# Half of the expert-row sum on TensorE, and expert 1's first weight chunks called in the routing stage

## The reference

```python
logits = (xt @ p['w_router'] + p['b_router']).astype(F32)
top_val, top_idx = lax.top_k(logits, TOP_K)                 # TOP_K = 4
gates = jax.nn.softmax(top_val, axis=-1)
...
def expert_block(args):
    e, x_b = args
    gu = x_b @ w_gu[e] + b_gu[e]
    gate = jnp.minimum(gu[..., ::2], SWIGLU_LIMIT)
    up = jnp.clip(gu[..., 1::2], -SWIGLU_LIMIT, SWIGLU_LIMIT)
    return ((up + 1.0) * (gate * jax.nn.sigmoid(SWIGLU_ALPHA * gate))) @ w_dn[e] + b_dn[e]
...
y = jnp.zeros((T + 1, D)).at[slot_tok].add(yb * slot_g[:, None])[:T]
```

## Time and profile before

| | us |
|---|---|
| median of 3 timed runs | 2890.73 |
| lowest, highest | 2877.65, 2892.95 |
| the profiled execution, its own time | 2882.36 |
| its span (first to last instruction) | 2880.6 |
| of it: expert turns, TensorE from 1167.3 to 2222.2 | 1054.8 |
| of it: the sum's stage, 2227.7 to 2280.3 | 52.5 |

### The profile page before, as it was taken

How to read it: one execution, slowest core, us unless ns; L and a number is a source line. 1 busy time by engine, 2 the same in 40 slices (tenths; PEclk the granted TensorE clock), 3 DMA queues, 4 the chain that set the end, 5 groups by cost and what they waited for, 6 DMA issues and landing times. The chain is left out here.

```text
span 2880.6 us, 62057 instructions
## 1 busy us (share of the span) xinstructions
PE 2493.6 (87%) x23388; PEld 1218.8 (42%) x23388; DVE 1253.4 (44%) x2324; ACT 694.8 (24%) x1558; POOL 453.0 (16%) x384
## 2 busy tenths in 40 slices
PE   5888888856889996799999998999898699789998
PEld 3456565645564443233333332333233254455444
DVE  2263747463257426344444444544454512643012
ACT  3133333343061013111111111121111411354000
POOL 0031213130070000211111111111110101154000
PEclk8998989878899997899999999999999699989999
DMA  6000000000308325799999999599987421001221
GB/s 256 27 28 25 6 25 6 4 2 32 111 8 332 135 73 209 272 423 424 424 424 424 423 424 423 221 424 423 423 339 286 157 88 69 20 3 66 73 73 58
DMA packets 114812, 552.07 MB, mean 192 GB/s; under 512 B 13633, under 2 KB 17217, under 8 KB 63202
## 3 DMA queue, kind: packets, MB, share of 16 engines
q1 hardware_dynamic: 97234, 510.79, 43.9%
q0 software_dynamic: 6912, 20.98, 1.9%
q10 hardware_dynamic: 10512, 18.08, 1.8%
HBM read 734.74 MB, written 16.52 MB: 261 GB/s over the span
## 5 line engine op out<-in xcount | busy, mean ns | idle before, releaser
L1517 PE MATMUL moe_gu_ps<-expert_w,xgT 128*32 128x512 f32 x6016 | 683.2, 601 | 62.0 <-PEq L1450 61.9
L1517 PEld LDWEIGHTS moe_gu_ps<-expert_w,xgT 128*32 128x32 f32 x6016 | 231.2, 111 | 496.7 <-issue 496.7
L1537 PE MATMUL moe_down_ps<-expert_w,actT 128*32 128x512 f32 x3008 | 346.3, 593 | 14.0 <-PEq L1450 14.0
L1438 ACT ACTIVATE xgT<-xt,ffn_shift,ffn_gain 128x64 f32<-128x64 f32 x384 | 137.6, 429 | 785.5 <-ACTq L1450 785.5
L1624 DVE COPY expert_w<-b_w 128x2048 f32 x188 | 231.7, 1233 | 171.6 <-DVEq L1450 158.7
L1537 PEld LDWEIGHTS moe_down_ps<-expert_w,actT 128*32 128x32 f32 x3008 | 114.2, 110 | 228.2 <-issue 227.3
L1631 DVE TENSOR_TENSOR biased<-moe_gu_ps,b_gu 128x1024 f32<-128x1024 f32 x47 | 57.6, 1225 | 250.1 <-DVEq L1450 250.1
L1429 POOL DMA_INDIRECT xg<-normed_rows,tokens x96 | 150.7, 1570 | 82.9 <-POOLq L1450 68.3
L1499 POOL COPY tokens<-token_of 128x2 uint32 x47 | 8.6, 182 | 816.0 <-POOLq L1450 816.0
L521 PE MATMUL b2p_ps<-b_w,b_hT 128*128 128x512 f32 (+1 forms) x320 | 121.3, 542 | 2.9 <-PEq L66 2.9
L521 PE MATMUL b2g_ps<-b_w,b_hT 128*128 128x512 f32 x256 | 111.7, 599 | 0.7 <-PEq L57 0.7
(11 more groups left out here) (593 smaller groups left out, 3587.1 us busy)
## 6 DMA issues: line engine op xcount, KB each, us to landing
expert_w<-in_w_experts SPq DMA_DIRECT2D x384, 1024.0 KB, 9.9
b_w<-in_w_experts SPq DMA_DIRECT2D x192, 1024.0 KB
late_w<-in_w_late SPq DMA_DIRECT2D x12, 2048.0 KB, 9.1
b_w<-in_w_in SPq DMA_DIRECT2D x10, 2048.0 KB, 7.5
begin_w<-in_w_ada SPq DMA_DIRECT2D x6, 2048.0 KB, 17.6
slot_rows<-yb ACTq DMA_DIRECT2D x94, 128.0 KB
mix_w<-in_w_in_tok SPq DMA_DIRECT2D x4, 2048.0 KB, 11.2
x<-in_w_rkv SPq DMA_DIRECT2D x4, 1536.0 KB, 6.5
```

What stands on the lines that cost most here:

```text
L1438: made = nc.scalar.activation(xgT[:, k, :, :], xt[:, :, k, :], ACT.Identity, scale=gain[:, k:k + 1], bias=shift[:, k:k + 1])
L1517: made = nc.tensor.matmul(ps_gu[UNIT * j:UNIT * j + UNIT, u, :], xgT[:, k, u, :], w[:, k, 512 * j:512 * j + 512], start=(k == 0), stop=(k ...
L1537: made = nc.tensor.matmul(ps_dn[to:to + UNIT, :], actT[:, u, c, :], w[:, i, at:at + 512], start=(c == 0), stop=(c == KD - 1), skip_group_c ...
```

## The change

Four edits:

1. The key of expert 1 is set to -0.5 (one more DVE instruction), so that it always follows expert 0.
2. The first four gate-up chunks of expert 1 are called in the routing stage: three right behind the store of the normed rows, ahead of the table's store; the fourth once the rows' store has landed. The spare places are now, in order, the two halves of `ring.slots[1]`, the last 1 MB piece of `expert_w` (the second half of the normed rows, which POOL has copied by then), and the first half of `ring.slots[0]`. `hot` moves to `hT`, whose contents are used up. The calls ahead of the loop of turns go.
3. The stage "moe_end" goes; its waits stand at the end of the lists of "moe", which now clears all of the semaphores.
4. In the sum DVE adds only the first two of the four rows of each token. ACT makes for the other two 8 diagonals of shares (`share_diag`), and TensorE multiplies them with the gathered rows into the bank where the biases are. The bias products of tile 0 move ahead of the diagonals' products.

```diff
-                for k in range(SPARES):
-                    load_spare(k, after, here)
...
                 sp.dma_start(rows.rearrange("(m p) n -> p m n", p=P), ...).then_inc(s["rows"], 16)
+                for k in range(3):
+                    weights.load_second(sp, k)
                 sp.wait_ge(s["expert"], 2)
                 sp.dma_start(table[0:1, :], experti[:, 0:1]).then_inc(s["table"], 16)
+                sp.wait_ge(s["rows"], 16)
+                weights.load_second(sp, 3)
                 sp.wait_ge(s["table"], 16)
-                sp.wait_ge(s["rows"], 16)
...
                 step(nc.vector.memset(key[:, 0:1], -1.0))
+                step(nc.vector.memset(key[:, 1:2], -0.5))
...
+        halves = [ring.slots[i][:, 4 * j:4 * j + 4, :].rearrange("p k n -> p (k n)") for i in (1, 0) for j in (0, 1)]
+        self.spare = [halves[0], halves[1], self.w[:, CHUNKS + 1, :], halves[2]]
...
+    def load_second(self, sp, k):
+        sp.dma_start(self.spare[k], self.source[1, k]).then_inc(self.spare_here[k], 16)
...
-        with stage(nc, "moe_end", "none", clear=arrived + carried) as (s, block):
...
+                act.wait_ge(stored, 32)
+                act.wait_ge(bias_here, 16)
...
+            pe.wait_ge(s["share_diag"], NT_X)
             for m in range(NT_X):
                 if m >= banks:
-                    pe.wait_ge(s["summed"], (m - banks) * TOP_K + 1)
...
+                    pe.wait_ge(s["summed"], (m - banks) * BY_VECTOR + 1)
+                if m:
+                    biases(m)
+                pe.wait_ge(arrived[m], 16 * TOP_K)
+                for j in range(BY_VECTOR, TOP_K):
+                    for c in range(2):
+                        last = nc.tensor.matmul(ps_b[:, m % banks, 512 * c:512 * c + 512],
+                                                share_diag[:, m, j - BY_VECTOR, :],
+                                                taken[:, m * TOP_K + j, 512 * c:512 * c + 512], start=False,
+                                                stop=(j == TOP_K - 1), skip_group_check=True)
...
-                for j in range(TOP_K):
+                for j in range(BY_VECTOR):
                     rows, share = taken[:, m * TOP_K + j, :], weight[:, m, j:j + 1]
-                    if j == 2 and m >= 2:
+                    if j == 1 and m >= 2:
                         inverse(1, m - 2)
```

More of the change, by code:

```diff
@@ L862, in ffn_block @@
         moving = ffn.enter_context(ExitStack())
-        weights = ExpertWeights(nc, d, moving)
+        weights = ExpertWeights(nc, d, moving, ring)
         y = weights.normed
@@ L878, in ffn_block @@
                         early=first_loads, first=make_affine, n_first=2)
-        route_stage(nc, tables, g, hT_next, ones, y, rows, weight, slot_of, of_expert, token_of, table, n_blocks,
-                    *ring.slots)
+        route_stage(nc, tables, weights, g, hT_next, ones, y, rows, weight, slot_of, of_expert, token_of, table, n_blocks,
+                    ring.slots[0])
         routing.close()
-        slot_rows = experts(nc, d, g, weights, ring, rows, gain, shift, token_of, table, n_blocks)
+        slot_rows = experts(nc, d, g, weights, rows, gain, shift, token_of, table, n_blocks)
         moving.close()
@@ L1130, in load, with route_stage @@
             sp.dma_start(to, source).then_inc(self.loaded, 16)
-def route_stage(nc, tables, g, hT, ones, xn, rows, weight, slot_of, of_expert, token_of, table, n_blocks, spare,
-                spare2):
+def route_stage(nc, tables, weights, g, hT, ones, xn, rows, weight, slot_of, of_expert, token_of, table, n_blocks,
+                spare):
     with ExitStack() as held:
@@ L1386, in load_first, with experts @@
             sp.dma_start(self.w[:, i], self.source[0, i]).then_inc(self.arrived[i], 16)
-def experts(nc, d, g, weights, ring, rows, gain, shift, token_of, table, n_blocks):
+    def load_second(self, sp, k):
+        sp.dma_start(self.spare[k], self.source[1, k]).then_inc(self.spare_here[k], 16)
+def experts(nc, d, g, weights, rows, gain, shift, token_of, table, n_blocks):
     ident = g.ident[:, :]
@@ L1399, in experts @@
     GU, DUMP = KD, CHUNKS
-    spare = [ring.slots[k // 2][:, 4 * (k % 2):4 * (k % 2) + 4, :].rearrange("p k n -> p (k n)") for k in range(SPARES)]
+    spare, spare_here = weights.spare, weights.spare_here
     with ExitStack() as held:
@@ L1483, in _ @@
                         load(i, here, before)
+                for here in [*spare_here, *arrived[SPARES:GU]]:
+                    sp.wait_ge(here, 16)
             @block.gpsimd
@@ L1701, in _, with biases @@
             last.then_inc(s["turned"], 1)
+            def biases(m):
+                for c in range(2):
+                    nc.tensor.matmul(ps_b[:, m % banks, 512 * c:512 * c + 512], of_expertT[:, m, :],
+                                     b_dn[:, 512 * c:512 * c + 512], start=True, stop=False, skip_group_check=True)
+            pe.wait_ge(s["kept"], 1)
+            pe.wait_ge(s["loaded"], 16)
+            biases(0)
             for i in range(2):
@@ L1753, in _ @@
                 .then_inc(s["kept"], 1)
+            for m in range(NT_X):
+                for j in range(BY_VECTOR, TOP_K):
+                    last = nc.scalar.activation(share_diag[:, m, j - BY_VECTOR, :], g.ident[:, :], ACT.Copy,
+                                                scale=weight[:, m, j:j + 1])
+                last.then_inc(s["share_diag"], 1)
             for i, to in enumerate((row, row2)):
```

32 lines of the change are left out of this document (11 added, 21 removed).

## The result

The kernel with the change takes **2892.23 us** (median of 20 executions, 2885.51 to 2906.1), the kernel before 2885.11 us (median of 20 beside it, 2874.49 to 2892.95). The ratio is 1.0024, with a 95% interval of 1.0013 to 1.0035: the change costs 3.8 to 10.1 us. The forecast was a gain of 1.0 us, and a time of 2888. The time lies in the range, and by the bound of 0.5% it is "no change", as forecast; but the sign is wrong: the interval excludes a gain. The rest of this document looks for the 7 us.

A forecast was written before the change was run, and what follows sets the result against it. No engine was taken to bound the whole span, so waits were read in three places. +0.2 - 0.2 - 1.0 = -1.0 us, giving 2881.4 from the profiled 2882.36 and 2889.7 or 2884.9 from other runs; 2888 taken, range 2876 to 2897.

The forecast's parts named there:

- Part 1: Key of expert 1: the order of experts stays, and the extra DVE instruction costs nothing.
- rival E: Expert turns: the order of experts changes, and waits for weights grow by 1 to 3 us each; 1%.
- Part 2, the routing's end: Routing's end: table queues behind three chunks, next stage 4.3 us later, gather gives back 4.1; sum +0.2 us.
- Rival A: Routing's end: the table doesn't wait for the chunks, gather gives up to 4.1 us; total -5, 2885; 12%.
- Part 2, the turns: Expert turns: earlier chunks gain nothing, the turns keep their pace, length unchanged at 1054.8 us.
- rival C: Expert turns: early chunks free the DMA engines, worth at most 9.9 us, 2878; 3%.
- Part 3: Seam behind the experts: without moe_end, one seam and fewer clears; -0.2 us, ends -0.5 and +0.2.
- Part 4: Sum of expert rows: start loses 1.3 us, the step to tile 1 regains 2.3; -1.0 us, ends -2.6 and +1.6.
- B: Sum of expert rows: TensorE stays at half clock while it sums; +20 us, total 2908; 4%.
- D: Sum of expert rows: TensorE's part is worth nothing or costs up to 2 us (late clock), 2890; 12%.

The follow-up runs named there:

- e3: The kernel before with only the early calls, the changed spare places and expert 1's key; ratio 1.0019 to the kernel before.
- e5: The kernel before with only the change's spare places, expert 1's key and one-hot tile, chunks called where they were before; ratio 1.0026.
- e12: The same kernel as e5, run once more beside the others; ratio 0.9996 to the kernel before.
- e14: e5 with the place behind the weights taken by the first spare chunk instead of the third; turns 1015.87 us.
- e11: e5 with the third spare place in the ring instead of the weights' own tensor; turns 1014.26 us.

## Why the prediction was wrong

**Where the 7 us are.** By the columns, means of all executions with a part against all without:

```
routing's end, chunks ahead of the table   62.36 (3) - 61.79 (8)     +0.6   forecast +0.2
turns, place in the weights' tensor        1015.70 (8) - 1014.46 (8) +1.2   forecast  0
last down products at half clock           8.77 (6) - 7.13 (10)     +1.6   forecast  0
gap behind the turns, no moe_end           6.03 (4) - 5.62 (12)      +0.4   forecast -0.2
sum by TensorE                             52.98 (6) - 54.08 (10)    -1.1   forecast -1.0
behind it, no moe_end and TensorE's sum    602.71 (3) - 599.12 (13)  +3.6   forecast  0
sum                                                                  +6.3   forecast -1.0
```

The timed runs give +6.9, with 3.8 to 10.1. That the columns come so near is in part luck: the first round (24.3 to 27.7 us) and the last column scatter by more than most of these terms.

**Part 1** (the order of experts stays): right, the turns have the same pattern of runs in before and after, and rival E is out.

**Part 2, the routing's end: right in mechanism and nearly in size.** The table queued behind the chunks and landed after 16.6 us (14.4 and 16.2 in the two others), forecast 14.6. Two terms were off: the rows landed 6.2 to 8.4 us behind the table's issue (7.0 taken), and the three chunks took another 7.8 to 8.8 us (7.5 taken). The 0.3 us from SP's wait to the barrier were an estimate from no row; DVE's copy came 1.65 us behind the landing, where it came 1.5 behind the end of DVE's work before, so they were 0.1. The loss at the stage's start was 5.1 us in the two profiles of the change and 2.4 in e3 (DVE's idle time 3.88 there), forecast 4.3; the gather gave back 4.0, forecast 4.1. Rival A is out. The forecast saw that the two cancel, and didn't ask for the version in which they don't: with the table first only the gain is left, -3.7 us in five executions (58.12 against 61.79).

**Part 2, the turns: the step that failed.** "Nothing is gained behind this ... The turns keep their pace" was argued for the calls, and for these it held (rival C is out). The other edit of that part, one spare place moved into the weights' own tensor, was not given a term at all: it was put at nothing without a reason. With it the stream of chunks was 0.17% slower and the turns 1.2 us longer, and in six of eight executions the last down products ran in part at half clock, 1.6 us. These 2.8 us are the largest part of the loss that runs isolated (e5, e12 and e14 against e11).

**Part 3: wrong in sign, outside its ends.** The forecast took 2.8 to 3.0 us from the last store's issue to its landing and 1.2 from there to the first work. ScalarE passed its waits 3.3 us behind the issue (2231.94 to 2235.2), and 1.5 followed: 4.8 instead of 4.3. The old kernel hid the landing under its first seam; the step knew that, and priced both what then stands in line and what follows it too low.

**Part 4: right, in mechanism and size.** -1.1 against -1.0. Two 32-row products at half clock took 3.74, the first sum of DVE came at 15.3 us (forecast 15.7), the clock came back at 2246.94, 4.3 us into the diagonals' products (4.0 forecast) and not already in the biases of tile 0, and stayed at 1.00 through the tiles; rivals B and D are out. The steps between the tiles came as forecast too: counted from the stage's first work, ScalarE's norms stand at 26.3, 34.1, 42.3 and 47.8 us in before and at 27.7, 33.3, 41.5 and 47.0 in after, so 1.4 us are lost at tile 0, 2.3 come back to tile 1, and the steps behind stay. One sum of the prediction doesn't add up: 2.3 products in 4.0 us and 1.7 at 0.86 make 5.5 us for the four that spread the diagonals, and it wrote 6.1 (2233.7 to 2239.8). They took 5.8.

**Behind: not seen.** The prediction ended at the next projection. A seam 180 us later became 0.3 us longer, and two rows of products behind it ran for longer at half clock. No row read from before told this; but that the prediction put the unchanged rest at exactly zero, with no ends, was a choice. The range of 2876 to 2897 held the time only because the draw of the executions had been given room.

## What to carry to other kernels

Put the small transfer that someone waits for ahead of the bulk on its queue: as soon as the 0.5 KB table stood before the early calls of weights, they cost nothing at the routing's end, and 3.7 us were gained. Give each edit of a change a term, the silent ones too (a buffer that moves, a stage that goes), and an uncertainty of a few microseconds to the unchanged stages of a kernel whose TensorE clock rises and falls. And read small effects from stretches between near events over several profiles, since a median of a dozen executions here has an interval of 5 us either way.

## What the runs showed of the hardware

- A 0.5 KB store landed 14.4 to 16.6 us after its issue with three 1 MB loads ahead of it on SP's queue, and 7.5 to 8.9 us after it with the loads behind it.
- A saturated stream of 1 MB loads, one in twelve of which goes to a place in another tensor of SBUF (same partitions, same packets), was 0.17% slower than with that place in the ring: 319.99 and 320.00 against 319.46 and 319.45 us for 135.31 MB. The rise is spread over many of its packets.
- One seam, the same code, took 1.65 us in twelve executions and 1.97 in the four with one stage less ahead of it; GpSimd took 0.3 us longer between its drain and its signal there.
- TensorE's granted clock fell to 0.50 shortly behind an idle time of 2.36 us in six executions, all with that spare place, and stayed at 1.00 behind the same idle time in ten; and behind 1.97 us in three, but not behind 1.98 in one. Where TensorE waited for transfers in any case, such a fall cost nothing.
